# The last expert unit's second column half: loaded in two halves of rows, its result split over two PSUM banks and copied and scattered by quarters of 256 columns

## What is computed

```python
def hierarchical_moe(h, norm_w, rg_w, rg_b, re_w, re_b, w_gate, w_up, w_down):
    xt = rms_norm(h, norm_w).reshape(-1, d)
    ...
    out = jnp.zeros_like(xt)
    for e in range(N_EXPERTS):
        he = jax.nn.silu(xt @ w_gate[e]) * (xt @ w_up[e])
        out = out + gates[:, e:e + 1] * (he @ w_down[e])

def reference(...):
    h = x
    for layer in range(DEPTH):              # DEPTH = 2
        ...                                 # h = h + mixer(h)
        h = h + hierarchical_moe(h, ...)
    return rms_norm(h, final_norm_w)
```

## Time and profile before

| | |
|---|---|
| time, median of 3 runs | 1295.76 us (1295.19 to 1295.98) |
| the profiled execution: its own time, its span | 1293.6 us, 1291.6 us |
| PE busy in the span | 1193.6 us (92%) |
| DVE, ACT, POOL busy | 280.2, 205.2, 32.4 us |
| moved by DMA, mean rate | 463.03 MB, 358 GB/s |
| rate in a slice of the expert stages | 424 to 428 GB/s in most |
| granted clock of PE, mean | 0.978 of full |

### The profile page before, as it was taken

How to read it: one execution, slowest core, us unless ns; L and a number is a source line. 1 busy time by engine, 2 the same in 40 slices (tenths; PEclk the granted TensorE clock), 3 DMA queues, 4 the chain that set the end, 5 groups by cost and what they waited for, 6 DMA issues and landing times.

```text
span 1291.6 us, 15079 instructions
## 1 busy us (share of the span) xinstructions
PE 1193.6 (92%) x6020; PEld 587.4 (45%) x6020; DVE 280.2 (22%) x681; ACT 205.2 (16%) x487; POOL 32.4 (3%) x42
## 2 busy tenths in 40 slices
PE   7999999999999999979598999999999999966686
PEld 6865775444444444533232466553444444422232
DVE  6741562141111111100000336241111111100001
ACT  2233232120000000000001336321000000000002
POOL 0001210000000000000000012000000000000000
PEclk9999999999999999999899999999999999998799
DMA  9930169589999999999999771689999999999996
GB/s 357 361 131 26 49 227 426 218 355 427 427 426 426 428 427 424 426 424 426 426 426 415 299 287 73 254 354 427 426 426 427 428 426 426 427 427 427 426 427 276
DMA packets 84728, 463.03 MB, mean 358 GB/s; under 512 B 7552, under 2 KB 9648, under 8 KB 36528
## 3 DMA queue, kind: packets, MB, share of 16 engines
q1 hardware_dynamic: 84656, 462.02, 86.7%
HBM read 460.91 MB, written 1.07 MB: 358 GB/s over the span
## 4 chain that ended last, share of the span: by engine, by line
PE 76%; DMA 11%; SPq 10%; DVE 1%; ACT 1%; issue 1%; DVEq 0%; ACTq 0%
PE bank L1608 22%; PE bank L420 15%; PE bank L1617 11%; SPq L273 7%; PE bank L1575 6%; DMA h<-in_w_down 5%; PE bank L1592 5%; PE bank L403 3%; PE bank L1952 3%; DMA own<-in_w_up 2%; DMA own<-in_w_gate 2%; SPq L1367 2%; PE bank L359 2%; PE bank L1639 1%; PE bank L388 1%; SPq L1373 1%
## 5 line engine op out<-in xcount | busy, mean ns | idle before, releaser
L1608 PE MATMUL bank<-own,work 128*64 128x512 f32 (+1 forms) x1112 | 264.7, 617 | 19.6 <-DMA own<-in_w_up 10.0
L1608 PE MATMUL bank<-late,work 128*32 128x512 f32 (+1 forms) x568 | 146.6, 614 | 7.9 <-DMA own<-in_w_up 7.9
L1617 PE MATMUL bank<-own,work 128*32 128x512 f32 (+1 forms) x480 | 125.4, 625 | 25.8 <-DMA h<-in_w_down 13.3
L1608 PEld LDWEIGHTS bank<-own,work 128*64 128x64 f32 (+1 forms) x1112 | 75.5, 127 | 148.2 <-issue 148.0
L1476 DVE TENSOR_TENSOR work<-work,bank 128x512 f32<-128x512 f32 x24 | 25.5, 1064 | 467.7 <-ACT work L1539 467.7
L1575 PEld LDWEIGHTS bank<-work,xs 128*128 128x128 f32 x736 | 85.6, 191 | 38.2 <-issue 38.2
L1539 ACT ACTIVATE work<-bank 128x512 f32<-128x512 f32 x24 | 14.3, 597 | 524.0 <-PE bank L1608 524.0
L1575 PE MATMUL bank<-work,xs 128*128 128x128 f32 x736 | 94.4, 281 | 0.0
L1592 PE MATMUL bank<-work 128*128 128x512 f32 x192 | 87.1, 595 | 3.0 <-DVE work L1481 1.6
L420 PE MATMUL bank<-xnT,own 128*128 128x256 f32 x384 | 84.7, 380 | 0.0
L420 PEld LDWEIGHTS bank<-xnT,own 128*128 128x128 f32 x384 | 72.3, 190 | 10.0 <-issue 0.4
(11 more groups left out here) (327 smaller groups left out, 1309.3 us busy)
## 6 DMA issues: line engine op xcount, KB each, us to landing
own<-in_w_up SPq DMA_DIRECT2D x78, 1024.0 KB, 26.5
own<-in_w_gate SPq DMA_DIRECT2D x61, 1024.0 KB, 26.0
own<-in_w_down SPq DMA_DIRECT2D x56, 1024.0 KB, 26.2
late<-in_w_gate SPq DMA_DIRECT2D x40, 1024.0 KB, 25.8
late<-in_w_up SPq DMA_DIRECT2D x31, 1024.0 KB, 26.8
late<-in_w_down SPq DMA_DIRECT2D x27, 1024.0 KB, 26.0
own<-in_a_in_w SPq DMA_DIRECT2D x17, 1024.0 KB, 13.7
h<-in_w_down SPq DMA_DIRECT2D x10, 1024.0 KB, 29.4
```

Of the source, the lines that this page charges most:

```text
L1608: ins = pe.matmul(bank[q * T:(q + 1) * T, :], self.xg[:, at:at + T], cut(tile(q), k=4)[:, k, :], start=(half == 0 and k == 0), stop=(half ...
L1617: ins = pe.matmul(self.b_down[out][q * T:(q + 1) * T, :], self.turned[:, at:at + T], cut(tile(q), j=2)[:, j, 512 * out:512 * out + 512], s ...
```

## The change

The load, the matmuls, the copy and the scatter of the last unit's second column half are cut smaller, in both layers:

- **Loads.** The second column half (columns 512 to 1023) of each of the four half-1 granules, one DMA of 512 KB before, becomes two of 256 KB: row j = 0 of all four granules first (`rows_loaded`), then row j = 1 of all four (`rest_loaded`). The number of bytes and of 2 KB runs stays the same; SP issues 8 DMAs in place of 4.
- **Down matmuls.** In the last unit the second column half's result goes to two banks: columns 512 to 767 to `b_down[1]`, columns 768 to 1023 to `b_gather` (which the last unit no longer needs). Half 0 of the last unit is split in the same way. In half 1, behind the scatter of the first column half, PE waits for `rows_loaded` and does j = 0 for both quarters, then waits for `rest_loaded` and does j = 1 for the first quarter (`quarter_down`), then for the second (`down_done`).
- **Copy and scatter.** DVE copies the two quarters one after the other (128 x 256 each), and PE scatters each behind its copy: 2 matmuls of 256 columns for each quarter. `scattered` is counted by those of the second quarter.
- Two semaphores of the first mixer get the names of two of the second mixer's (`mk_ev` and `mv_ev` become `kT_ev` and `kv_ev`), so that the two stages share them.

The rename stands in one row below; the other lines that carry it are left out.

```diff
@@ -672,7 +672,7 @@
-    names = ("x_act x_dve xT_ev dt_dve dt_act conv_dve conv_act z_ev q_ev m_act m_dve memT_ev mk_ev mv_ev xtok_ev bt_ev "
+    names = ("x_act x_dve xT_ev dt_dve dt_act conv_dve conv_act z_ev q_ev m_act m_dve memT_ev kT_ev kv_ev xtok_ev bt_ev "
...
@@ -1244,7 +1244,7 @@
 class Experts:
 
     MAIN = ("pick gated gathered xg_ready silu_done hid_ready turned turned_ready down_done gates_turned gates_ready y_ready "
-            "out_done y1_ready rest_loaded half_summed scattered ordered side_done side_ev")
+            "out_done y1_ready rows_loaded rest_loaded quarter_down half_summed scattered ordered side_done side_ev")
     OVER = ("pick gated gathered xg_ready gu_done silu_done hid_ready turned turned_ready down_done gates_turned gates_ready "
             "y_ready scattered gu0_loaded gu1_loaded down0_loaded down1_loaded")
     PAIRS = NE // 2
@@ -1278,13 +1278,13 @@
         _, _, u, what, half, q = job
         return self.weights(quad[UNITS_OF[u][0]] * IN_QUAD + (UNITS_OF[u][1] + q), what, half)
 
-    def in_two(self, job):
+    def in_pieces(self, job):
 
 
         return job[0] == "expert" and job[2:5] == (NU - 1, "down", 1)
 
-    def column_half(self, job, out):
-        return cut(self.c.slot(job), j=2)[:, :, 512 * out:512 * out + 512]
+    def by_rows(self, job):
+        return cut(self.c.slot(job), j=2)
 
     def released(self, job):
 
@@ -1362,15 +1362,15 @@
                 if place not in quad:
                     quad[place] = self.quad_of(sp, place)
                 sp.wait_ge(*self.released(before(job)))
-                if self.in_two(job):
-                    for_half, src = self.column_half(job, 0), self.job_source(job, quad)
-                    sp.dma_start(for_half, src[:, :, 0:512]).then_inc(c.w_loaded[JOB_AT[job][0]], 16)
+                if self.in_pieces(job):
+                    sp.dma_start(self.by_rows(job)[:, :, 0:512], self.job_source(job, quad)[:, :, 0:512]).then_inc(c.w_loaded[JOB_AT[job][0]], 16)
                 else:
                     c.load_job(sp, job, self.job_source(job, quad))
             most = self.beyond(sp)
-            for job in jobs:
-                if self.in_two(job):
-                    sp.dma_start(self.column_half(job, 1), self.job_source(job, quad)[:, :, 512:1024]).then_inc(s["rest_loaded"], 16)
+            for j, loaded in enumerate((s["rows_loaded"], s["rest_loaded"])):
+                for job in jobs:
+                    if self.in_pieces(job):
+                        sp.dma_start(self.by_rows(job)[:, j, 512:1024], self.job_source(job, quad)[:, j, 512:1024]).then_inc(loaded, 16)
 
             def body(rnd, p, n):
                 sp.wait_ge(o["scattered"], n + 1)
@@ -1477,9 +1477,14 @@
                 if not last:
                     dve.wait_ge(s["gathered"], u * 2 + 4)
                     gathered(0, s["xg_ready"])
-                dve.wait_ge(s["down_done"], u * 2 + 2)
-                dve.tensor_copy(self.y[1][:, :], self.b_down[1][:, :]).then_inc(s["y1_ready"], 1)
-                if not last:
+                if last:
+                    dve.wait_ge(s["quarter_down"], 1)
+                    dve.tensor_copy(self.y[1][:, 0:256], self.b_down[1][:, 0:256]).then_inc(s["y1_ready"], 1)
+                    dve.wait_ge(s["down_done"], u * 2 + 2)
+                    dve.tensor_copy(self.y[1][:, 256:512], self.b_gather[:, 256:512]).then_inc(s["y1_ready"], 1)
+                else:
+                    dve.wait_ge(s["down_done"], u * 2 + 2)
+                    dve.tensor_copy(self.y[1][:, :], self.b_down[1][:, :]).then_inc(s["y1_ready"], 1)
                     dve.wait_ge(s["gathered"], u * 2 + 5)
                     gathered(1, s["xg_ready"])
 
@@ -1586,10 +1591,10 @@
                     ins = pe.transpose(self.b_turn[:, t * P:(t + 1) * P], cut(self.gated, t=NT)[:, t, :], c.f("ident"))
                 ins.then_inc(signal, 1)
 
-            def scatter(outs=(0, 1), each=None):
+            def scatter(outs=(0, 1), each=None, at=slice(0, 512)):
                 for out in outs:
                     for t in range(NT):
-                        ins = pe.matmul(self.sums[2 * t + out][:, :], self.gates_T[:, t * P:(t + 1) * P], self.y[out][:, :],
+                        ins = pe.matmul(self.sums[2 * t + out][:, at], self.gates_T[:, t * P:(t + 1) * P], self.y[out][:, at],
                                         start=False, stop=True, skip_group_check=True)
                         if each:
                             ins.then_inc(each, 1)
@@ -1609,13 +1614,16 @@
                                         start=(half == 0 and k == 0), stop=(half == 1 and k == 3))
                 return ins
 
-            def down(half, T, tile, outs=(0, 1)):
-                for out in outs:
-                    for j in range(2):
+            whole = [(self.b_down[0], 0, 512), (self.b_down[1], 512, 1024)]
+            split = [whole[0], (self.b_down[1], 512, 768), (self.b_gather, 768, 1024)]
+
+            def down(half, T, tile, pieces=whole, rows=(0, 1)):
+                for bank, a, b in pieces:
+                    for j in rows:
                         for q in range(P // T):
                             at = (2 * half + j) * P + q * T
-                            ins = pe.matmul(self.b_down[out][q * T:(q + 1) * T, :], self.turned[:, at:at + T],
-                                            cut(tile(q), j=2)[:, j, 512 * out:512 * out + 512],
+                            ins = pe.matmul(bank[q * T:(q + 1) * T, a % 512:a % 512 + b - a], self.turned[:, at:at + T],
+                                            cut(tile(q), j=2)[:, j, a:b],
                                             start=(half == 0 and j == 0), stop=(half == 1 and j == 1))
                 return ins
 
@@ -1678,24 +1686,36 @@
                     for q in range(P // T):
                         c.wait_job(pe, ("expert", layer, u, "down", half, q))
                     tile = lambda q: c.slot(("expert", layer, u, "down", half, q))
+                    pieces = split if last else whole
                     if half == 0:
-                        down(half, T, tile).then_inc(s["down_done"], 1)
+                        down(half, T, tile, pieces).then_inc(s["down_done"], 1)
                     else:
-                        down(half, T, tile, (0,)).then_inc(s["out_done"], 1)
+                        down(half, T, tile, pieces[:1]).then_inc(s["out_done"], 1)
                         if last:
                             pe.wait_ge(s["y_ready"], u + 1)
                             pe.wait_ge(s["gates_ready"], u + 1)
                             scatter((0,)).then_inc(s["half_summed"], 1)
+                            pe.wait_ge(s["rows_loaded"], 16 * (P // T))
+                            down(half, T, tile, pieces[1:], (0,))
                             pe.wait_ge(s["rest_loaded"], 16 * (P // T))
-                        down(half, T, tile, (1,)).then_inc(s["down_done"], 1)
+                            down(half, T, tile, pieces[1:2], (1,)).then_inc(s["quarter_down"], 1)
+                            down(half, T, tile, pieces[2:], (1,)).then_inc(s["down_done"], 1)
+                        else:
+                            down(half, T, tile, pieces[1:]).then_inc(s["down_done"], 1)
                 if not last:
                     pe.wait_ge(s["xg_ready"], u * 2 + 4)
                     gather(1, s["gathered"])
                     pe.wait_ge(s["y_ready"], u + 1)
                     pe.wait_ge(s["gates_ready"], u + 1)
                     scatter((0,))
-                pe.wait_ge(s["y1_ready"], u + 1)
-                scatter((1,), s["scattered"] if last else None)
+                if last:
+                    pe.wait_ge(s["y1_ready"], u + 1)
+                    scatter((1,), at=slice(0, 256))
+                    pe.wait_ge(s["y1_ready"], u + 2)
+                    scatter((1,), s["scattered"], slice(256, 512))
+                else:
+                    pe.wait_ge(s["y1_ready"], u + 1)
+                    scatter((1,))
 
             wait_cleared(pe)
             pe.wait_ge(router.s["n2_act"], 3 * NT)
```

More of the change, by code:

```diff
@@ L742, in freed @@
                     "xtok": (s["xtok_ev"], i + 1), "bt": (s["bt_ev"], 1), "ac": (s["ac_dve"], 2), "z": (s["z_ev"], i + 1),
-                    "q": (s["q_ev"], i + 1), "memT": (s["mem1_dve"], i + 1), "mk": (s["mk_ev"], i + 1),
-                    "mv": (s["mv_ev"], i + 1), "cb": (s["cb_dve"], i + 1),
+                    "q": (s["q_ev"], i + 1), "memT": (s["mem1_dve"], i + 1), "mk": (s["kT_ev"], i + 1),
+                    "mv": (s["kv_ev"], i + 1), "cb": (s["cb_dve"], i + 1),
                     "sc": (s["sm_act"], 2 * i + 2), "pT": (s["pt_ev"], i + 1), "pv": (s["pv_ev"], i + 1),
@@ L896, in _ @@
                     U.wait_done(act, key)
-                    act.activation(cut(mkT, h=4)[:, i, :], bank[:, 0:256], ACT.Copy).then_inc(s["mk_ev"], 1)
```

(7 more changed lines are left out.)

## The result

The changed kernel took 1297.86 us (median of 22 executions, 1295.84 to 1300.25); the kernel before, on the same chip, 1296.02 (22 executions, 1294.71 to 1300.75). The ratio is 1.0015, 95% interval 1.0009 to 1.0021: 1.8 us slower by the medians, where 2.45 us faster were forecast and the range ended at 1295.3. The profiled execution took 1298.89 us.

The account below looks back on a forecast made before the run. It took full DMA engines to bound the expert stages, so only the tails behind each layer's last landing could shrink: 1.2 us (layer 1) + 1.25 (layer 0) = 2.45 off 1295.76, giving 1293.3 us, range 1292.4 to 1295.3.

Parts of the forecast that it names:

- Half 0 of the unit gets more instructions and the same columns: Last unit's first half, down matmuls: the split adds instructions but no columns; no time was charged for it.
- PE's queue holds the next instructions: The new waits on PE add little, since its next instructions are already queued and nobody else stands behind them.
- the whole gain passes: From layer 0's end into the next mixer: it starts off the scatter, so all of layer 0's gain reaches the end.
- the slower rival: Rival 3, the only rival whose case was slower: 1300.1 us in all, chance 0.06.
- Layer 0's gain: Tail at layer 0's end: earlier matmuls and a shorter copy, less j = 0 running past the landing; 1.25 us.
- Layer 1's gain: Tail at layer 1's end, to DVE's sum: 1.31 us sooner less 0.15 for the landing, said as 1.2 us.
- The charge of 0.15 us for the landing: Layer 1's last landing: twice the transfers, at 0.04 us each for four more, make it 0.15 us later.
- The sum: Both layers' ends together: 1.2 + 1.25 = 2.45 us off the median 1295.76, giving 1293.3 us.
- Rival 1: Layer 1's last landing comes later, four more transfers costing 1.6 us; only layer 0 gains: 1294.8 us, chance 0.20.
- Rival 2: Narrow matmuls of 256 columns cost as much as of 512, 0.43 us a step: 1296.0 us, chance 0.05.
- Rival 3: Both layers' last landings: an exposed fixed 0.9 us per added transfer moves each by 3.6 us: 1300.1 us, chance 0.06.
- Rival 4: Nothing shows, as a lagging DMA engine or the clock moves the end back as much: near 1295.7 us, chance 0.06.

Follow-up runs that it names:

- e2: The change put into layer 0 alone, against the kernel before: ratio 1.0018.
- e8: The changed kernel run again unchanged, against the kernel before: ratio 1.0020.
- e6: The kernel before with 24 matmuls (96 instructions) that never run, added in layer 0 inside the block PE jumps over: ratio 1.0041, median 1300.10 us.
- e14: The kernel before with 15 small matmuls (60 instructions) added at PE's start: ratio 1.0031.
- e7: The changed kernel with 16 small matmuls (64 instructions, full weights) added at PE's very start: ratio 1.0008 against the kernel before.
- e9: The changed kernel with 12 cheaper matmuls (48 instructions, 32 columns of weights) added at PE's start: ratio 1.0006 against the kernel before.
- e13: The changed kernel with 24 small matmuls (96 instructions) added at PE's start: ratio 0.9975 against the kernel before, median 1293.02 us.
- e4: The kernel before, run again unchanged as a yardstick: ratio 0.9998.
- e1: The change put into layer 1 alone, against the kernel before: ratio 0.9992, median 1295.51 us.
- e10: The kernel before with loads by rows in both layers and the quarter banks, copies and scatters in layer 1 alone: ratio 0.9984, median 1293.93 us.
- e3: The kernel before with loads by rows in both layers, but still one bank, one copy and one scatter: ratio 0.9989, median 1295.19 us.
- e5: The kernel before with 12 matmuls (48 instructions) that never run, added in layer 0 inside the block PE jumps over: ratio 1.0029, median 1299.28 us.
- e12: The kernel before with 3 matmuls (12 instructions) that never run, added in layer 0 inside the block PE jumps over: ratio 1.0012.

## Why the prediction was wrong

**The step that failed** is the one on instructions: "Half 0 of the unit gets more instructions and the same columns", priced at nothing, as the renamed semaphores were, and beside it "PE's queue holds the next instructions". For the time on PE's datapath that holds. But 72 more instructions ahead of the branch in layer 0 moved its target over a fetch edge; behind the branch PE's queue did not hold the next instructions, and that cost 4.0 to 4.5 us (scatter to q 9.45 to 9.95 in place of 5.44): 2.8 us of stall behind the copies of the sums (6.51 less 3.67), and the rest at the half clock. In e2 and e8 q's own 16 rows took another 0.5 us, 7.54 and 7.56 in place of 7.03, in e6 and e14 1.1 and 1.3 us. So "the whole gain passes" into layer 1 failed too: the copies were earlier by the gain, but what came next was no longer them. None of the rivals was this one; the slower rival had the right sign and the wrong place, so nothing in the prediction covers the result.

**Layer 0's gain, 1.25 us:** right, as far as the scatter's start. From the last landing to the scatter it is 2.79 us in before (at unit + 16.65 and + 19.44) and 1.56 to 1.57 in after, e2, e8, e7 and e9: 1.23 sooner. PE went from j = 0 to j = 1 with no idle time in after and e2, as forecast; in e13 it waited 0.79 us there. Counted from the unit, the changed kernel's own profile hides this: its first column half let PE start at unit + 12.7, against + 11.6 before.

**Layer 1's gain, 1.2 us:** right in its steps, too large for the changed kernel as it ran. From the last landing to the scatter it is 2.78 us in before and e4 and 1.23 in e1 and e10, 1.55 sooner, as the prediction has it. ACT's second square stands 4.80 us behind that landing in e4 and 3.48 in e1: 1.32 sooner, forecast 1.31. The idle time ahead of j = 1, forecast near 1 us, was 0.34 and 0.33 us in e1 and e10, and in after, e8, e7, e9 and e13 there was none: there the landing of the first column half bounds the tail, the second square stands 3.94 us behind the last landing in after, and 0.86 us is gained. The charge of 0.15 us for the landing isn't seen.

**The sum, 2.45 us:** near without the stall; e13 measured 2.7 us by the medians (2.1 to 4.5 by the ratio's interval). Part of that agreement is luck. In the profiles of e7, e9 and e13 layer 1's last landing is at unit + 16.28 or + 16.29, some 1 us sooner than in e4 or e1. The kernel before has this too in one profile (e6: + 16.25, scatter at + 19.04), and against that their scatter at + 17.86 is only 1.2 us sooner. For the changed kernel the parts give 4.2 (scatter to q 9.61 in place of 5.44) less 1.2 less 0.9, 2.1 us slower, and 1.8 was measured. Of the two ends alone, e1 is 1.1 us faster by the runs. The lower end of the range doesn't follow from its words: 1293.3 less 0.3 and 0.8 is 1292.2, not 1292.4.

**Rival 1, a later landing:** fell. The last landing in layer 1 was at unit + 17.11 with eight transfers (e1, e3), + 17.27 with four (e4). **Rival 2, narrow steps at 0.43:** fell, 0.22. **Rival 3, an exposed fixed part of each transfer:** fell by the same landings; its 0.9 us a transfer would have moved them by 3.6. (What the prediction cites of the Trainium skill there is on transfers that GpSimd issues; here SP issues them.) **Rival 4:** the change did show.

**Left open.** In both profiles of the unpadded changed kernel the first column half of layer 1's last unit let PE start at unit + 12.3 and + 12.7, where the other profiles have + 11.2 to + 11.3, so that the scatter there was at + 18.9 and + 19.3, that is 1.7 us behind the last landing, where e1 has 1.23. This takes about a third of layer 1's gain back. In layer 0 such starts also came to kernels without the change (e6 + 12.3, e14 + 12.5), so I take it for chance there. For layer 1, whether the stall 550 us earlier shifts something, or chance did it twice, no run tells; e9, with the stall and the change, has + 11.3. Nor does a run tell why the last landing came 1 us sooner in e6, e7, e9 and e13.

## What to carry to other kernels

Where a kernel branches over code that doesn't run, count instructions as well as work: added ones ahead of the branch, or in the skipped block, may cost several microseconds without one more being waited for. The sign is an "issue" wait right behind the branch, with no releaser, that ends just behind an instruction packet (1.6 to 1.7 us here), and a halved clock after it. Tell it from a wait of the change's own by putting never-run instructions into the skipped block of the kernel before; cure it by shifting the program (24 tiny matmuls at the start did it here), and measure a change again in a shifted place before it is judged.

## What the runs showed of the hardware

- A jump of PE over a block that had not been fetched held it until 6.05 to 6.5 us after the scatter's start, 1.60 to 1.71 us behind the end of an instruction packet, beside a data queue at 400 GB/s. The packet itself started 3.47 to 3.95 us after the scatter's start and took 0.9 us. Without the stall PE went on after 3.66, when DVE's copies were done. The transposes behind it took 3.15 to 3.65 us at a granted clock of 0.50, where they otherwise take 1.94.
- Instructions that never run cost 0.29% (e5), by their place alone.
- Where the target's block was there and the one behind it came late (e12), it showed as 0.4 us of issue at the next group of matmuls, again 1.60 us behind the packet's end, not at the branch.
- A pad of 32 columns of weights and 8 of data costs little at the start: 24 of them from 3.51 us for 2.73 us, first real matmul at 7.69. With 128 columns of weights, 16 took 7.00 us, and the first real matmul came at 10.34.
